# Second feed-forward network of a decoder layer in 7 block products instead of 8

## The reference

```python
x = x + 0.5 * _swiglu(_rms_norm(x, g[0]), W['ffa_up'], W['ffa_down'])
# three sequence mixers on one projection of rms(x): RWKV7, mLSTM, sparse attention
x = x + jnp.concatenate([o_rw, o_ml, o_nsa], axis=-1) @ W['w_out']
x = x + _mem_attend(_rms_norm(x, g[2]), st['mem_kv'], W['mem_w_q'], W['mem_qk_g'][0], W['mem_w_o'])
x = x + 0.5 * _swiglu(_rms_norm(x, g[4]), W['ffb_up'], W['ffb_down'])

def _swiglu(h, w_up, w_down):
    gate, up = jnp.split(h @ w_up, 2, axis=-1)
    return (jax.nn.silu(gate) * up) @ w_down
```

## Time and profile before

| | us |
|---|---|
| runs, median of 3 (lowest, highest) | 3831.72 (3829.81, 3835.63) |
| profiled execution, first to last instruction (span) | 3827.4 |
| median of the runs less that span: what lies around it | 4.3 |
| first matmul of the second network | 2752.65 |
| its last piece of matmuls ends, modelled | 3810.46 |

### The profile page before, as it was taken

The page is one execution under the profiler, slowest core; times in us unless marked ns, Lnnn a source line. Parts: engine busy times, 40 slices in busy tenths (PEclk is TensorE's granted clock), DMA queues, the critical chain, the costliest instruction groups (busy, mean ns, idle before and its releaser), DMA issues. The chain is left out here.

```text
span 3827.4 us, 44331 instructions
## 1 busy us (share of the span) xinstructions
PE 3565.6 (93%) x18084; PEld 2313.9 (60%) x18084; DVE 1295.4 (34%) x3074; ACT 564.3 (15%) x1261; POOL 180.2 (5%) x282
## 2 busy tenths in 40 slices
PE   7999899999999999997987968988899999999998
PEld 4666565666567777665665734444565556656776
DVE  3445603223312223314543458743432122111111
ACT  1000011000011101012223426630110001000000
POOL 3111100000000000000001100000000000000000
PEclk8999999999999999997687869999999999999999
DMA  6565554232234332335335431031043342233443
GB/s 158 178 190 169 169 143 117 87 97 75 88 111 118 102 98 71 101 121 112 43 82 157 141 99 55 7 124 39 12 124 91 96 119 80 76 98 110 124 128 91
DMA packets 607237, 401.76 MB, mean 105 GB/s; under 512 B 90636, under 2 KB 584060, under 8 KB 602556
## 3 DMA queue, kind: packets, MB, share of 16 engines
q1 hardware_dynamic: 578956, 314.10, 30.0%
q0 software_dynamic: 13824, 67.12, 5.6%
q10 hardware_dynamic: 14256, 17.71, 1.3%
HBM read 367.95 MB, written 36.13 MB: 106 GB/s over the span
## 5 line engine op out<-in xcount | busy, mean ns | idle before, releaser
L412 PE MATMUL psum<-arena 128*128 128x384 f32 (+1 forms) x4224 | 1335.2, 474 | 21.0 <-DVE arena L547 11.8
L412 PEld LDWEIGHTS psum<-arena 128*128 128x128 f32 x4224 | 798.8, 192 | 488.1 <-issue 25.1
L422 PE MATMUL psum<-arena 128*128 128x384 f32 (+1 forms) x2112 | 661.3, 472 | 0.0
L422 PEld LDWEIGHTS psum<-arena 128*128 128x128 f32 x2112 | 399.5, 191 | 234.9 <-issue 4.1
L445 PE MATMUL psum<-arena 128*128 128x384 f32 (+3 forms) x816 | 273.5, 492 | 6.0 <-DVE arena L547 6.0
L499 ACT ACTIVATE arena<-psum 128x384 f32<-128x384 f32 (+1 forms) x132 | 62.4, 472 | 1173.9 <-PE psum L412 1173.5
L561 DVE SCALAR_TENSOR_TENSOR arena<-arena,psum 128x384 f32<-128x384 f32 (+1 forms) x132 | 70.1, 531 | 473.6 <-ACT arena L499 472.0
L445 PEld LDWEIGHTS psum<-arena 128*128 128x128 f32 (+1 forms) x816 | 154.3, 193 | 103.7 <-issue 27.3
L570 DVE TENSOR_TENSOR arena<-psum,arena 128x384 f32<-128x384 f32 (+1 forms) x132 | 70.7, 535 | 333.4 <-PE psum L412 327.0
L577 DVE SCALAR_TENSOR_TENSOR arena<-psum,arena 128x384 f32<-128x384 f32 (+1 forms) x96 | 51.3, 535 | 362.4 <-PE psum L422 359.8
L454 PE MATMUL psum<-arena 128*128 128x264 f32 (+3 forms) x576 | 137.0, 399 | 0.0
(11 more groups left out here) (558 smaller groups left out, 3279.5 us busy)
## 6 DMA issues: line engine op xcount, KB each, us to landing
arena<-in_ffa_up SPq DMA_DIRECT2D x132, 512.0 KB, 5.2
arena<-in_ffb_up SPq DMA_DIRECT2D x132, 512.0 KB, 5.0
arena<-in_ffa_down SPq DMA_DIRECT2D x48, 704.0 KB, 4.4
arena<-in_ffb_down SPq DMA_DIRECT2D x48, 704.0 KB, 4.5
arena<-in_w_in SPq DMA_DIRECT2D x27, 1024.0 KB, 5.9
arena<-in_w_in SPq DMA_DIRECT2D x9, 1056.0 KB, 5.6
pT<-arena ACTq DMA_DIRECT2D x32, 192.0 KB, 5.4
arena<-xs SPq DMA_DIRECT2D x2, 2176.0 KB, 19.3
```

Of the source, the lines that this page charges most:

```text
L412: ins = mm(b[:, 0:n], w[:, g, k], hC[:, k, 0:n], start=(k == 0), stop=(k == KD - 1))
L422: ins = mm(b[:, 0:n], w[:, k], actT[:, k, 0:n], start=(k == 0), stop=(k == FH - 1))
```

## The change

The network's matrix product is cut in blocks of 2 x 2 and made by Strassen's scheme in Winograd's form: 7 block products. A is the weights, B the activations. In the up part a group is one tile of 128 inner columns: A11, A12 are the two halves (4 tiles each) over the width of the gate's weights, A21, A22 those of the up weights; B11, B21 are the two width halves of the first half of the chunk's tokens, B12, B22 those of the second. So a product is 4 matmuls on 192 (160) tokens. In the down part the inner width goes in four passes of 2, 3, 3 and 3 pairs of tiles, with 4 groups behind each pass, each for two output tiles; a product is 2 or 3 matmuls. A chunk is 38 groups, in `FFB`.

The sums of weights S1 = A21 + A22, S2 = S1 - A11, S4 = A12 - S2, S3 = A11 - A21 are made by GpSimd for each group (`ffb_gp`), in two buffers `sums_w`, the last one in place of A21. The sums of activations T1 = B12 - B11 (in place), T2 = B22 - T1, T3 = B22 - B12, T4 = B21 - T2 are made by VectorE: for the up part once a chunk (`h_sums_dve`), for the down part with each pair of up groups. Group m's products are issued as P1 (A11 B11), then the last product (A22 T4) of group m-1, P5 (S1 T1), P6 (S2 T2), P2 (A12 B21), P3 (S4 B22), P7 (S3 T3). They accumulate in three PSUM regions x, y, z; where a region is accumulated on further, ScalarE (up: `snap`) or VectorE (down: straight to `xT`) reads it before. Weights come as `gate_w` (2 buffers) and `lift_w` (3 buffers), a DMA of 512 KB each (down: 384 or 256). `yrow` has two tiles instead of three, and some buffers are laid elsewhere to make room. The norm's sums of chunks 1 and 2 use bank 5, which they share with the attention. First network and mixers keep their work.

```diff
+        def mem_bank(pe):
+            rv = pe.ring(mem_v)
+            pe.wait_ge(rv.read, rv.freed())
+            if pe.late_sums:
+                pe.wait_ge(sums_read, pe.late_sums)
+            return rv.next()
...
-        arena.at = dense_end + 3 * D
-        MX = [hC.rearrange("p k c -> p (k c)"),
-              yrow.rearrange("p s (h c) -> p (s h) c", h=2).rearrange("p a c -> p (a c)"),
-              actT.rearrange("p k c -> p (k c)")]
-        MX = [MX[c][:, 0:KD * CH[c][1]].rearrange("p (k c) -> p k c", k=KD) for c in range(3)]
+        HW = PIECE // 2
+        late_a = Arena(arena.array, dense_end - KD * 8 - 2 * PIECE)
+        late_a.at = sample_at
+        hB = late_a.take(P, KD, PIECE)
+        gate_w, lift_w = late_a.take(P, 2, D), late_a.take(P, 3, D)
+        hT = late_a.take(P, 3, KD // 2 * HW).rearrange("p t (k c) -> p t k c", k=KD // 2)
+        act_at = late_a.at
+        actB = late_a.take(P, 6, PIECE)
+        aT = [late_a.take(P, 3, HW)]
+        snap = late_a.take(P, 3, HW)
+        tg = late_a.take(P, 2, HW)
+        late_b = Arena(arena.array, size)
+        late_b.at = dense_end - KD * 8
+        aT += [late_b.take(P, 3, HW) for _ in range(2)]
+        yrow = late_b.take(P, 2, D)
+        arena.at = late_b.at
...
             sp.wait_ge(mem_keys_made, 1)
-            load_slab(sp, 3 * LOADS_A)
-            load_slab(sp, 3 * LOADS_A + 1)
+            for m in range(2):
+                load_lift(sp, m)
+                load_gate(sp, m)
...
             scale_dve(v, 4, 0)
+            h_sums_dve(v, 0)
...
+        PASSES = [(0, 2), (2, 5), (5, 8), (8, 11)]
+        FFB = []
+        for c in range(3):
+            for q, (a, z) in enumerate(PASSES):
+                FFB += [("up", c, q, f) for f in range(2 * a, 2 * z)]
+                FFB += [("down", c, q, p) for p in range(KD // 2)]
...
+        def load_gate(sp, m):
+            kind, c, q, x = FFB[m]
+            if m >= 2:
+                sp.wait_ge(products_made, PRODUCTS[m - 2, "P2"])
+                sp.wait_ge(weights_summed, GATHERS + m - 1)
...
+        def load_lift(sp, m):
+            kind, c, q, x = FFB[m]
+            if m >= 3:
+                sp.wait_ge(products_made, PRODUCTS[m - 3, "last"])
...
+        def ffb_gp(gp):
+            gp.wait_ge(out_v[2], 9 + NB + 2 * KD)
+            for m in range(len(FFB)):
+                w = left_of(m)
+                gp.wait_ge(gate_in[m % 2], GATE_0 + 16 * (m // 2 + 1))
+                gp.wait_ge(lift_in[m % 3], LIFTS_0[m % 3] + 16 * (m // 3 + 1))
+                if m >= 2:
+                    gp.wait_ge(products_made, PRODUCTS[m - 2, "P3"])
+                gp.eng.tensor_tensor(w["S1"], w["A21"], w["A22"], ALU.add).then_inc(gpsimd_done, 1)
+                gp.wait_ge(gpsimd_done, gp.done(gpsimd_done))
+                gp.eng.tensor_tensor(w["S2"], w["S1"], w["A11"], ALU.subtract).then_inc(gpsimd_done, 1)
+                gp.wait_ge(gpsimd_done, gp.done(gpsimd_done))
+                gp.eng.tensor_tensor(w["S4"], w["A12"], w["S2"], ALU.subtract).then_inc(gpsimd_done, 1)
+                gp.wait_ge(gpsimd_done, gp.done(gpsimd_done))
+                gp.eng.tensor_tensor(w["S3"], w["A11"], w["A21"], ALU.subtract).then_inc(weights_summed, 1)
+                gp.wait_ge(weights_summed, GATHERS + m + 1)
...
+        def product(pe, out, left, right, first=True):
+            n = left.shape[1]
+            for k in range(n):
+                ins = pe.eng.matmul(out, left[:, k], right[:, k], start=(first and k == 0), stop=(k == n - 1), skip_group_check=True)
+            ins.then_inc(products_made, 1)
+        def last_pe(pe, m):
+            pe.wait_ge(evacuated, EVACUATED[m, "u2" if FFB[m][0] == "up" else "P7"])
+            if FFB[m][0] == "up":
+                pe.wait_ge(h_summed, GATHERS + 4 * FFB[m][1] + 4)
+            else:
+                pe.wait_ge(act_summed, GATES_0 + 4 * pair_number(m) + 4)
+            product(pe, x_bank(m), left_of(m)["A22"], right_of(m)["T4"], first=False)
+        def ffb_pe(pe, c):
+            for m in range(chunk_end(c - 1) + 1, chunk_end(c) + 1):
+                A, B = left_of(m), right_of(m)
+                up, u, j = FFB[m][0] == "up", up_number(m), pair_number(m)
+                x, y, z = x_bank(m), y_bank(m), z_bank(m)
+                if m > chunk_end(c - 1) + 1:
+                    pe.wait_ge(evacuated, EVACUATED[m - 1, "g2" if FFB[m - 1][0] == "up" else "P3"])
+                else:
+                    pe.wait_ge(h_made, pe.due(h_made, KD))
+                    if m:
+                        pe.wait_ge(evacuated, EVACUATED[m - 1, "P3"])
+                pe.wait_ge(weights_summed, GATHERS + m + 1)
+                product(pe, x, A["A11"], B["B11"])
+                if m:
+                    last_pe(pe, m - 1)
+                if not up:
+                    pe.wait_ge(act_summed, GATES_0 + 4 * j + 3)
+                if up:
+                    pe.wait_ge(h_summed, GATHERS + 4 * c + 3)
+                product(pe, z, A["S1"], B["T1"])
+                yield
+                if up:
+                    pe.wait_ge(snaps_made, PROJS_0 + 3 * u + 1)
+                else:
+                    pe.wait_ge(evacuated, EVACUATED[m, "P1"])
+                product(pe, x, A["S2"], B["T2"], first=False)
+                if m:
+                    pe.wait_ge(evacuated, EVACUATED[m - 1, "last"])
+                product(pe, y, A["A12"], B["B21"])
+                if up:
+                    pe.wait_ge(snaps_made, PROJS_0 + 3 * u + 2)
+                else:
+                    pe.wait_ge(evacuated, EVACUATED[m, "P5"])
+                product(pe, z, A["S4"], B["B22"], first=False)
+                if up:
+                    yield
+                    pe.wait_ge(snaps_made, PROJS_0 + 3 * u + 3)
+                else:
+                    pe.wait_ge(evacuated, EVACUATED[m, "P6"])
+                product(pe, x, A["S3"], B["T3"], first=False)
...
+            for m in range(chunk_end(c - 1) + 1, chunk_end(c) + 1):
+                if FFB[m][0] == "down":
+                    yield
+                    continue
+                before = up_before(m)
+                act.wait_ge(products_made, PRODUCTS[m, "P1"])
+                if before is not None:
+                    act.wait_ge(evacuated, EVACUATED[before, "a2"])
+                a.copy(snap[:, 0, 0:h], x_bank(m)).then_inc(snaps_made, 1)
+                act.wait_ge(products_made, PRODUCTS[m, "P5"])
+                a.copy(snap[:, 1, 0:h], z_bank(m)).then_inc(snaps_made, 1)
+                yield
+                act.wait_ge(products_made, PRODUCTS[m, "P6"])
+                a.copy(snap[:, 2, 0:h], x_bank(m)).then_inc(snaps_made, 1)
+                act.wait_ge(evacuated, EVACUATED[m, "g1"])
+                a.activation(tg[:, 0, 0:h], snap[:, 0, 0:h], ACT.Tanh, scale=0.5).then_inc(tanhs_made, 1)
+                act.wait_ge(evacuated, EVACUATED[m, "g2"])
+                a.activation(tg[:, 1, 0:h], snap[:, 2, 0:h], ACT.Tanh, scale=0.5).then_inc(tanhs_made, 1)
+                yield
...
+        def h_sums_dve(v, c):
+            e, h = v.eng, half_of(c)
+            b11, b12, b21, b22 = hB[:, 0:4, 0:h], hB[:, 0:4, h:2 * h], hB[:, 4:8, 0:h], hB[:, 4:8, h:2 * h]
+            t2, t3, t4 = (hT[:, t, :, 0:h] for t in range(3))
+            v.wait_ge(h_made, v.counts[h_made.name])
+            e.tensor_tensor(t3, b22, b12, ALU.subtract).then_inc(h_summed, 1)
+            e.tensor_tensor(b12, b12, b11, ALU.subtract).then_inc(h_summed, 1)
+            v.wait_ge(h_summed, GATHERS + 4 * c + 2)
+            e.tensor_tensor(t2, b22, b12, ALU.subtract).then_inc(h_summed, 1)
+            v.wait_ge(h_summed, GATHERS + 4 * c + 3)
+            e.tensor_tensor(t4, b21, t2, ALU.subtract).then_inc(h_summed, 1)
...
+            kind, c, q, x = FFB[m]
+            h, X = half_of(c), x_bank(m)
+            v.wait_ge(products_made, PRODUCTS[m, "last"])
+            if kind == "down":
+                to_x(v, m, "last", 1, 0, X)
+                return
+            b11, b12, b21, b22, t2, t3, t4 = act_tiles(m)
+            v.eng.tensor_tensor(b21 if x % 2 else b11, X, tg[:, 0, 0:h], ALU.mult).then_inc(evacuated, 1)
+            if x % 2:
+                v.wait_ge(evacuated, EVACUATED[m, "last"])
+                v.eng.tensor_tensor(t4, b21, t2, ALU.subtract).then_inc(act_summed, 1)
+        def to_x(v, m, name, row, col, src):
+            _, c, q, p = FFB[m]
+            h, c0 = half_of(c), CH[c][0]
+            x = xT[:, 2 * p + row, c0 + col * h:c0 + (col + 1) * h]
+            v.wait_ge(products_made, PRODUCTS[m, name])
+            v.eng.scalar_tensor_tensor(out=x, in0=src, scalar=0.25, in1=x, op0=ALU.mult, op1=ALU.add).then_inc(evacuated, 1)
...
+        def ffb_dve(v, c):
+            e, h = v.eng, half_of(c)
+            c0, n = CH[c + 1] if c < 2 else (0, 0)
+            s1, s5, s2 = (snap[:, i, 0:h] for i in range(3))
+            t1, t2 = tg[:, 0, 0:h], tg[:, 1, 0:h]
```

(53 more changed lines are left out.)

308 lines of the change are left out of this document (201 added, 107 removed).

## The result

| | before | after |
|---|---|---|
| median of the runs (12 each, taken together) | 3828.93 us | 3838.19 us |
| lowest, highest | 3816.78, 3836.98 | 3828.27, 3847.59 |
| profiled execution, span | 3827.4 | 3826.6 |
| first to last matmul of the second network | 2752.65 to 3810.5: 1057.8 | 2744.37 to 3809.4: 1065.0 |
| of it chunk 0, 1, 2 (each from its first product to the next one's) | 376.2, 394.6, 287.0 | 383.2, 405.2, 276.6 |

The ratio is 1.0023 with a 95% interval of 1.0012 to 1.0033: slower by 9 us. The time forecast, 3820 us, was 18 us short; the range held it, the sign was wrong. The profiled execution of after is the fastest of its 12: it came to the last stage 11.4 us earlier than the one of before. From there to the end of the span it took 1297.9 us against 1287.3, +10.6, which fits the medians; all that follows is about that stretch.

What follows compares the result with a forecast made beforehand. TensorE's matmul issue was taken to bound the second network. Terms -113.1 + 27.7 + 27 + 5 + 25 + 8 + 4 + 3 + 2 = -11.4 us took the span from 3827.4 to 3816.0; with 4.3 added, 3820 us, range 3768 to 3875.

Steps and rivals of the forecast that it cites:

- the sign: Whole kernel, changed against before: faster was given 0.54, same 0.15, slower 0.31.
- Term a: TensorE's matmul issue in the second network: 852.3 us for 965.4, so -113.1 us.
- Term b: Group heads: TensorE waits for gate weights to be loaded and summed by GpSimd, +27.7 us.
- Term c: First down group's P5 waits for VectorE's sums, held up by GpSimd's: 12 x 2.25, +27 us (7 to 40).
- others keep up: Rival: VectorE slips its operations between GpSimd's and attention hides as before; 3771 us, chance 0.26.
- Terms d and e: VectorE held up at odd up groups, +5 us, and by interleaved attention in chunks 0 and 1, +25 us.
- term d: GpSimd's sums hold `last_dve` of odd up groups beyond the next group's P2, 21 places: +5 us (0 to 18).
- Terms f, g, h: Next chunk's scaling and sums in the last pass, +8 us; network's start, +4; network's end, +3.
- h: Network's end: third copy waits for the first store, last product has nothing between; +3 us (0 to 6).
- Term i: TensorE's clock falls only near the few longest waits: +2 us (0 to 20).
- The base: Whole kernel: the median of the runs was taken as 4.3 us above the profiled span.

Runs made afterwards that it cites:

- e2_fill: The changed kernel with GpSimd's four sums per group replaced by four fills of about the same length that read nothing: 3768.1 us, 0.984.
- e3: The changed kernel without the attention on memory tokens for chunks 1 and 2: 3701.0 us, 0.965.
- e4: The kernel before without the attention on memory tokens for chunks 1 and 2: 3743.3 us, 0.977.
- e1: The changed kernel with GpSimd's four sums per group left out, GpSimd only passing the signal on: 3740.0 us, 0.976.
- e7: The changed kernel with each group's last product directly behind its own P7, in front of the next group's P1: 3876.4 us, 1.014.
- e8: The changed kernel with three more small matmuls at the head of each down pass, where TensorE waits for VectorE: 3832.2 us, 1.002.

## Why the prediction was off

**Term a (-113.1): right.** 855.3 us of issue against 852.3, pitches of 163 and 136 ns to the digit.

**Term b, the load-and-sum loop (+27.7): right, for partly other reasons.** Measured 25 by distances, 23.1 of it idle time in ten waits. GpSimd's sums of 512 columns take at least 1.26 us (S1, S3) and 1.09 (S2, S4), with medians of 1.29, 1.27, 1.28 and 1.09 and 1.26 forecast, and a gate lands in 3.8 us with 3.9. But a third of the sum is the one load of 9.56 us at 2819.31, which I hadn't foreseen: it goes out beside two 1 MB cache loads of the attention. The other nine waits are of 0.2 to 4.9 us, 14 together, less than the loop was given; and the tight last chunk gave 276.6 us, with 273 forecast.

**Term c, heads of down passes (+27): right in place, number and cause, a little large.** Measured 21.0 in 12 waits, 1.75 us each for 2.25; tb3, b12 and tb2 each held until a sum of GpSimd's ends, as walked through. That is the rule of the Trainium skill, SBUF — State Buffer, Who interferes with whom: VectorE with two SBUF inputs and a GpSimd instruction that reads SBUF exclude each other. The trace agrees with 1.05, 1.14 and 0.91 us for 0.36, but here as in rows 9 the listed spans of the two overlap in part. The rival *others keep up* had this term at 7, and is close to what e2_fill shows once GpSimd stops reading: it forecast 3771 us, e2_fill has 3768. So the rival's premise was wrong and its sum right.

**Terms d and e, odd up groups and attention (+30): right in size, wrong in place.** Waits of 29 to 30 us were measured, but I had put them in front of the network's products, and only 4.4 us are there: two behind the attention's squares (L4472) and 0.3 us at one of the 21 places of term d, which so was next to nothing. The other 25 us are eight waits of the attention's own matmuls for VectorE's and ScalarE's rounds. That the sum came out is in part luck. What the attention costs the change in all is e3 and e4: 42 us gained without it, 9 lost with it.

**Terms f, g, h (+8, +4, +3):** 8.7 measured at the next chunk's scaling and sums; the start is 3.1 us longer (212.6 to 215.7); the tail is 16.9 and 17.2 us, so h was next to 0, inside its bounds. Small waits of another 6 to 7 us stood in no term.

All waits together: 82.3 us in the network, 6.4 in the others and 3.4 at the start and the end, 92.1 against 99.7 forecast.

**Term i, the clock (+2): this is the step that failed.** It measured +22 under the network's products and 6.5 more under the attention's, 28.5 in all, above its bound of 20 too. Between the -11.4 forecast and the +10.6 measured lie 22 us: 26.5 from this term and 3.3 from term a, less 7.6 by which the waits came out smaller. I took one window with 5 of 20 us idle and a clock of 0.91 as a case that only the few longest waits come near. In after there are 17 low stretches of 3.4 to 10.2 us, 77 us of 1065, where before has one of 7. Sixteen of the 17 lie at a single wait of 1.9 to 8.8 us, at the start, the heads, the attention's waits, the scaling and the loads; the wait at 3008.64, of 1.93 us, stands in a stretch otherwise fully busy. It doesn't always come so: of the 21 waits of 1.9 us or more, five, of 1.9 to 2.5 us, had no low stretch behind them, the one of 1.93 us in the timeline above (3095.01) among them. The seventeenth stretch follows no wait at all:
```profile
3330.00:3337.00 7.00, 7.00 (x31) 7.00 (x31) 0.36 (x1) 0.00 (x0) 0.00 (x0) 0.51 0.00 0
```
It begins within 64 matmuls of the attention on 32 columns each, and the only one of before (3310.85) begins within the same 64: this one the change did not bring. The price of the others is not in rows 2's mean: at the low level each network instruction takes up to 100 ns more, 1.3 us for the 13 of the 3.4 us stretch at 3009. I had counted the waits well and priced their aftermath at next to nothing.

Experiments agree without proving it alone: where the long waits go (e1, e2) low clock goes from 77.1 to 15.7 and 34.1 us, and where waits grow in number but not in length (e7) it falls to 49.8. A run with the waits and without the clock's drop could not be made (e8 tried); so that the 28.5 us would all come back stays worked out from the trace.

**The base.** The 4.3 us added to the span were too much. The profiled execution of after has a total of 3828.3 us for its span of 3826.6, 1.7 more, and the other runs show 1.7 to 1.9; the 3831.7 came from three runs, and twelve gave 3828.9. From there -11.4 makes 3817.5, and the miss is 21 us, not 18.

## What to carry over

When a change takes work off the bounding engine and leaves it waiting, price each long new wait with what the clock may take after it, not with its own length alone. Here that was 16 of the 21 waits of 1.9 us or more, and 28.5 us on top of some 92 us of waits; you have counted them already in walking through the terms. Before giving work to an idle GpSimd, look at which VectorE operations read two SBUF tiles on the path at that moment: a fill of the same duration in its place tells contention from occupation in one run. And what order alone gave back (P1 ahead of the sums' wait, the sums behind the chain, the loads elsewhere) was here 60 us, where the change as first made lost 9.
